# Upper parts first, pages split one by one, and one branch turned early: joined waits of an fp32 two-block transformer kernel on TensorE

## What is computed

```python
# block 1, layer i: HGRN2 + convolution mixer, then a feed-forward part
x = x + hybrid_mixer(rms_norm(x, norm_mix[i]), w_in[i], ...)
h = rms_norm(x, norm_ffn[i])
x = x + (swiglu(h, w1, w3, w2) if i == 0 else moe_swiglu(h, router_w, w1, w3, w2))  # 8 experts, 2 per token
# block 2, layer i
z = rmsnorm(x, norm_g[i]) @ w_in[i]
a = softmax(qk_0) - lam * softmax(qk_1)          # differential attention (branch A)
o_a = rmsnorm(a @ v, subln_g) * (1 - lam_init)   # needs the squares of the outcome
o_b = attention over the keys that an index picks (branch B)
o_c = gates * (compressed, selected, windowed attention) (branch C)
branches = [o_a * silu(a_g), o_b * silu(b_g), o_c * silu(c_g)]
x = x + sum(sigmoid(merge) * (branches @ w_up[i])) @ w_out[i]
x = x + (p[i] @ w_ple[i]) * sigmoid(rmsnorm(x, ple_norm_g[i]) @ w_ple_gate[i])
```

## Time and profile before

| | |
|---|---|
| median of 3 runs | 2567.53 us (2566.06 to 2570.06) |
| profiled execution | 2567.37 us, its span 2565.7 us |
| mean granted TensorE clock | 0.987 |
| TensorE busy | 2499.5 us, 17625 matmuls |
| VectorE busy | 1594.3 us |
| ScalarE busy | 1259.9 us |
| HBM read | 557.38 MB, mean 218 GB/s |

### The profile page before, as it was taken

One profiled execution on the slowest core, in us unless ns is written; L12 is line 12 of the kernel. 1 busy time (PEld: TensorE's weight loads), 2 busy tenths in 40 slices (PEclk: granted clock), 3 DMA queues, 4 the chain that ended last, 5 costly groups with the idle time before them and its releaser, 6 DMA issues.

```text
span 2565.7 us, 40739 instructions
## 1 busy us (share of the span) xinstructions
PE 2499.5 (97%) x17625; PEld 2205.2 (86%) x17625; DVE 1594.3 (62%) x1718; ACT 1259.9 (49%) x1286; POOL 5.4 (0%) x22
## 2 busy tenths in 40 slices
PE   8999999999999899999999999999999999999998
PEld 8999989989999787888887877878788898788997
DVE  5776655456766789889523334233555878557776
ACT  5555434355553576767423223233445565445555
POOL 0000000000000000000000000000000000000000
PEclk9999999999999899999999999999999999999999
DMA  7544455545442899999899789798356325555332
GB/s 240 181 164 149 141 188 182 189 165 179 160 139 91 331 391 336 350 339 363 292 335 322 262 311 342 241 334 320 132 181 193 106 89 174 181 164 172 103 119 95
DMA packets 308482, 561.07 MB, mean 219 GB/s; under 512 B 11024, under 2 KB 121040, under 8 KB 308304
## 3 DMA queue, kind: packets, MB, share of 16 engines
q1 hardware_dynamic: 307296, 556.36, 63.3%
q10 hardware_dynamic: 1008, 2.11, 0.2%
HBM read 557.38 MB, written 1.05 MB: 218 GB/s over the span
## 4 chain that ended last, share of the span: by engine, by line
PE 91%; DVE 6%; ACT 1%; issue 1%; DMA 0%; DVEq 0%; ACTq 0%
PE psG L713 61%; PE psX L713 13%; PE psG L1055 5%; PE psG L1076 2%; DVE ring_rest L2213 2%; PE psG L1378 1%; PE psG L961 1%; PE psX L1295 1%; PE psX L825 1%; PE psG L1349 1%; PE psX L702 1%; ACT tops L1509 1%; PE psX L847 0%; PE psG L1103 0%; PE psX L1246 0%
## 5 line engine op out<-in xcount | busy, mean ns | idle before, releaser
L2213 DVE TENSOR_TENSOR ring_rest<-ring,tops 128x2048 fp32r<-128x2048 f32 (+1 forms) x255 | 580.2, 2288 | 262.3 <-ACT tops L1509 260.4
L1509 ACT ACTIVATE tops<-ring 128x2048 fp32r<-128x2048 f32 (+1 forms) x255 | 483.4, 1907 | 164.5 <-PE psG L713 160.4
L713 PE MATMUL psG<-hT_rest,tops 128*128 128x256 f32 x1728 | 491.8, 285 | 0.0
L713 PE MATMUL psG<-hT_top,ring_rest 128*128 128x256 f32 x1632 | 465.2, 285 | 0.0
L713 PE MATMUL psG<-hT_top,tops 128*128 128x256 f32 x1376 | 397.9, 289 | 8.2 <-DVE hT_rest L2129 6.9
L1509 ACT ACTIVATE arena<-psG 128x512 f32<-128x512 f32 (+2 forms) x166 | 100.9, 608 | 585.7 <-PE psG L713 371.0
L713 PEld LDWEIGHTS psG<-hT_rest,tops 128*128 128x128 f32 x1728 | 334.1, 193 | 0.6
L713 PEld LDWEIGHTS psG<-hT_top,ring_rest 128*128 128x128 f32 x1632 | 315.9, 194 | 0.0
L713 PEld LDWEIGHTS psG<-hT_top,tops 128*128 128x128 f32 x1376 | 266.7, 194 | 10.9 <-DVE hT_rest L2129 7.3
L2213 DVE TENSOR_TENSOR ring_rest<-ring,tops_more 128x2048 fp32r<-128x2048 f32 x93 | 211.9, 2288 | 34.6 <-ACT tops_more L1509 34.1
L713 PE MATMUL psG<-tops,hT_top 128*128 128x512 f32 (+1 forms) x480 | 189.0, 394 | 5.4 <-issue 3.2
(11 more groups left out here) (467 smaller groups left out, 5139.7 us busy)
## 6 DMA issues: line engine op xcount, KB each, us to landing
ring<-in_expert_w_dram SPq DMA_DIRECT2D x180, 1024.0 KB, 7.3
ring<-in_w_in_dram SPq DMA_DIRECT2D x136, 1024.0 KB, 5.2
arena<-in_expert_w_dram SPq DMA_DIRECT2D x117, 1024.0 KB, 6.7
ring<-in_dense_w_dram SPq DMA_DIRECT2D x33, 1024.0 KB, 5.3
ring<-in_w_out_dram SPq DMA_DIRECT2D x16, 1024.0 KB, 5.0
ring<-in_w_up_dram SPq DMA_DIRECT2D x12, 1024.0 KB, 5.0
ring<-in_w_proj_conv_dram SPq DMA_DIRECT2D x8, 1024.0 KB, 5.1
ring<-in_w_proj_hgrn_dram SPq DMA_DIRECT2D x8, 1024.0 KB, 5.1
```

The lines of the kernel that those rows point to most:

```text
L713: mm = pe.matmul(dst, left[a], right[c], start=start and n == 0, stop=stop and n == 2)
L1509: act.activation(dst, src, func, **kw).then_inc(S[name], 1)
L2213: dve.tensor_tensor(part_of_page(rest_of(p), cols), part_of_page(raw(p), cols), part_of_page(top_of(PG.top[n]).bitcast(F32), cols), ALU.su ...
```

## The change

It has these parts:

1. The first product behind a norm goes by passes: all upper x upper products of the tile first (these wait for `hT_topped` and, for a page, `topped` alone), then the passes that need `hT_parted` or `parted` (`by_passes`, `up_first`, `tile_by_halves`).
2. In the broad jobs the three products of a page are issued page by page instead of piece by piece, with `upper_part` (waits `topped`) ahead of `both` (waits `parted`), for the g and u pages as for the down pages.
3. `top(n0)` and `rest(n0)`, the first expert page, stand between the two gathers.
4. `lead` is 2, 3, 4, 5 from tiles (1,0), (1,1), (1,2) on, instead of 2 and then 5 from (1,0).
5. `top_hT(3, ...)` and `parts(3, ...)`, the split of the activations for the 22 last steps, stand in tiles c = 3, 4 of the last broad job instead of 4, 5.
6. `mix_maps` folds one scaling into another and has no marker copy at its end (`maps_mixed` counts 2 per unit); the squares of A outcomes are read from PSUM by ScalarE (`squares_of_maps`, semaphore `o_squares`, for which `values` of the next unit waits), and the compressed keys and values are copied by ScalarE.
7. Branch A is turned, rounded and split within the last unit: TensorE ahead of the last gate tile, ScalarE ahead of `top(m+13)`, VectorE behind `rest(m+13)` and ahead of `outcome` of unit 14.

```diff
-            return 2 if n < expert_page("t", 1, 0, 0) else TOP_SLOTS - 1
+            return 2 + sum(n >= expert_page("t", j, c, 0) for j, c in ((1, 0), (1, 1), (1, 2)))
...
+            def upper_part(n, cols):
+
+                pe.wait_ge(S["topped"], PG.part[n])
+                return top_of(PG.top[n]).rearrange("p (a b) -> p a b", b=cols)
...
+            def by_passes(banks, page_n, n, norm):
+
+                for left, right in ((0, 0), (1, 0), (0, 1)):
+                    if right:
+                        pe.wait_ge(S["hT_parted"], part_of_h(norm, 2 + n))
+                    elif not left:
+                        pe.wait_ge(S["hT_topped"], part_of_h(norm, 2 + n))
+                    w = both(page_n, W)[1] if left else upper_part(page_n, W)
+                    for c in range(4):
+                        for kk in range(4):
+                            at = 4 * n + kk
+                            mm = pe.matmul(two(banks[:, c // 2, T * (c % 2):T * (c % 2) + T]), w[:, kk, P * c:P * c + P], hTp[right][:, :, at, :],
+                                           start=at == 0 and c % 2 == 0 and left == right == 0, stop=at == KD - 1 and c % 2 == 1 and right == 1)
+                return mm
...
                     if norm is not None:
-                        pe.wait_ge(S["hT_parted"], part_of_h(norm, 2 + n))
+                        mm = by_passes(psG[:, b], n0 + n, n, norm)
+                        mm.then_inc(used, 1)
+                        if mid and n == 0:
+                            mid()
+                        continue
...
+                        if j == part == 0:
+                            up_first(w)
+                            continue
...
+                def up_first(w):
+
+                    for left, right in ((0, 0), (1, 0), (0, 1)):
+                        for g in range(2):
+                            pe.wait_ge(S["hT_parted" if right else "hT_topped"], part_of_h(1, 2 + g))
+                            for c in range(2):
+                                for k in range(4 * g, 4 * g + 4):
+                                    mm = pe.matmul(two(psG[:, 0, 0, T * c:T * c + T]), w[left][:, k, P * c:P * c + P], hTp[right][:, :, k, :],
+                                                   start=left == right == k == c == 0, stop=right == c == 1 and k == KD - 1)
+                    mm.then_inc(used, 1)
...
+                            n = expert_page("t", j, c, part) + g
+                            if c == 0 and part == 0:
+                                pe.wait_ge(S["m_gath"], 2 * j + g + 1)
+                            w = upper_part(n, cols)
+                            for kk in range(per):
+                                k = per * g + kk
+                                pe.matmul(psG[:, 0, part, 0:cols], g_top[:, j % 2, k, :], w[:, kk, :], start=k == 0, stop=False)
                             if c == 0 and part == 0:
                                 pe.wait_ge(S["m_gpart"], 2 * j + g + 1)
-                            w = both(expert_page("t", j, c, part) + g, cols)
+                            for kk in range(per):
+                                pe.matmul(psG[:, 0, part, 0:cols], g_rest[:, j % 2, per * g + kk, :], w[:, kk, :], start=False, stop=False)
+                            w = both(n, cols)[1]
                             for kk in range(per):
                                 k = per * g + kk
-                                mm = three(psG[:, 0, part, 0:cols], (g_top[:, j % 2, k, :], g_rest[:, j % 2, k, :]),
-                                           [v[:, kk, :] for v in w], k == 0, k == KD - 1)
+                                mm = pe.matmul(psG[:, 0, part, 0:cols], g_top[:, j % 2, k, :], w[:, kk, :], start=False, stop=k == KD - 1)
...
+            def turn_branch(l, b):
+                pe.wait_ge(S["branch_on"], 2 * l + (2 if b == 1 else 1))
+                for c in range(4):
+                    for h in range(TH):
+                        dst = psXc[:, 4 * b + c, :] if b < 2 else psG4[:, c, :]
+                        col = (A_G, B_G, C_G)[b] + P * c
+                        mm = pe.transpose(dst[:, P * h:P * h + P], zt[:, h, col:col + P], ident)
+                mm.then_inc(S["bT_psum"], 1)
...
                     turn_exps(l, n)
+                    if n == N_UNITS - 1:
+                        turn_branch(l, 0)
                     gate_tile(l, *divmod(HALVES[n] + (n in DOUBLE), 2))
                     values(l, n)
...
                 gathered(0, 0, slim_ps)
+                top(n0)
+                state[0] += 1
                 gathered(0, 1, slim_out)
...
-                        if j == BROAD - 1 and c in (4, 5):
+                        if j == BROAD - 1 and c in (3, 4):
                             act.wait_ge(S["m_scat"], 4 * j)
-                            top_hT(3, c - 4)
+                            top_hT(3, c - 3)
...
+            def squares_of_maps(l, n):
+
+                _, qh, cs = UNITS[n]
+                act.wait_ge(S["av_read"], N_UNITS * l + n + 1)
+                for c in range(2):
+                    do(o_tmp[:, P * c:P * c + P], av_ps[:, P * c:P * c + P], ACT.Square, "o_squares",
+                       accum_out=lg[:, 9, 4 * qh + cs[c]:4 * qh + cs[c] + 1])
...
                     turned_read(l, n)
                     if n + 1 < N_UNITS:
                         softmax(l, n + 1)
+                    if n == 0:
+                        act.wait_ge(S["cmp_out"], l + 1)
+                        do(kcT[:, :, 0:NCMP], cmp_k[:, :, 0:NCMP], ACT.Copy, "cmp_sb")
+                        for c in range(4):
+                            do(vbd[32 * c:32 * c + 32, c, :], cmp_v[32 * c:32 * c + 32, c // 2, :], ACT.Copy, "cmp_sb")
                     k = PAIR_OF_STEP.get(n)
                     if n == N_UNITS - 1:
+                        branch_tops(l, 0)
                         top(m + k + 2)
                     if k:
                         gates_read(l, k)
                     if k and n < N_UNITS - 1:
                         top(m + k + 2)
+                    if UNITS[n][0] == "A":
+                        squares_of_maps(l, n)
...
                 step(dve.reciprocal(r, den[:, n % 2, 0:4]))
-                step(dve.tensor_scalar(r[:, 2:4], r[:, 2:4], nlam[:, l:l + 1], None, ALU.mult))
                 for c in range(2):
-                    go(dve.tensor_scalar(sv[:, 2 + c, :], sv[:, 2 + c, :], r[:, 2 + c:3 + c], None, ALU.mult))
+                    go(dve.tensor_scalar(sv[:, 2 + c, :], sv[:, 2 + c, :], r[:, 2 + c:3 + c], nlam[:, l:l + 1], ALU.mult, ALU.mult))
                 own()
                 for c in range(2):
                     go(dve.scalar_tensor_tensor(out=sv[:, c, :], in0=sv[:, c, :], scalar=r[:, c:c + 1], in1=sv[:, 2 + c, :],
-                                                op0=ALU.mult, op1=ALU.add))
-                own()
-                step(dve.tensor_copy(st[:, 10:11], eps), "maps_mixed")
+                                                op0=ALU.mult, op1=ALU.add), "maps_mixed")
 
             def outcome(l, n):
                 kind, qh, cs = UNITS[n]
                 k = len(cs)
                 if kind == "A":
-                    o, t = av_ps[:, 0:T].rearrange("p (c d) -> p c d", d=P), o_tmp[:, 0:T].rearrange("p (c d) -> p c d", d=P)
+                    o = av_ps[:, 0:T].rearrange("p (c d) -> p c d", d=P)
                     gated = zt[:, qh, A_G + P * cs[0]:A_G + P * cs[0] + T].rearrange("p (c d) -> p c d", d=P)
                     dve.wait_ge(S["branch_gates"], 4 * l + 4)
                     dve.wait_ge(S["av_full"], N_UNITS * l + n + 1)
-                    go(dve.tensor_copy(t, o))
-                    go(dve.tensor_tensor(gated, gated, o, ALU.mult))
-                    own()
-                    step(dve.tensor_tensor(t, t, o, ALU.mult), "av_read")
-                    step(dve.tensor_reduce(lg[:, 9, 4 * qh + cs[0]:4 * qh + cs[0] + 2], t, AX_X, ALU.add))
...
+            def branch_rests(l, i):
+                b = BRANCHES[i]
+                dve.wait_ge(S["bT_topped"], 3 * l + i + 1)
+                go(dve.tensor_tensor(b_rests[b], psXc[:, 4 * b:4 * b + 4, :] if b < 2 else psG4,
+                                     b_top[:, 4 * b:4 * b + 4, :].bitcast(F32), ALU.subtract), "bT_parted")
...
-                dve.wait_ge(S["cmp_out"], l + 1)
-                step(dve.tensor_copy(kcT[:, :, 0:NCMP], cmp_k[:, :, 0:NCMP]), "cmp_sb")
...
                     if n == N_UNITS - 1:
                         rest(m + 13)
+                        branch_rests(l, 0)
```

More of the change, by code:

```diff
@@ L78 @@
 DOUBLE = (0, 3, 6, 7, 10, 13, 14)
+BRANCHES = (0, 2, 1)
 ROUNDS = {5: (0, 1), 6: (1, 2), 7: (2, 4), 8: (4, 6), 10: (6, 8)}
@@ L2551, in experts @@
                 gathered(0, 0, slim_ps)
+                rest(n0)
+                state[0] += 1
                 gathered(0, 1, slim_out)
@@ L2570, in experts @@
                             slots(j + 1)
-                        if j == BROAD - 1 and c in (4, 5):
```

(3 more changed lines are left out.)

64 lines of the change are left out of this document (29 added, 35 removed).

## The result

The changed kernel takes 2557.68 us (median of 13 runs, 2551.04 to 2561.96), the kernel before in the same runs 2571.24 us (2565.23 to 2577.74): a ratio of 0.9947, 95% interval 0.9934 to 0.9960. It is faster by 13.6 us. The forecast was 20.3 us less, 2547, with a range up to 2557.0; it missed that range by 0.7 us. 3.8 us of the distance lie in the base, which the sum took as 2567.4 us; the other 6.7 lie in the terms.

A forecast was written before the change was run, and what follows sets the result against it. TensorE, busy 2499.5 of 2565.7 us, bounds the kernel, so only its waits and low-clock stretches can be won. Terms sum to 20.3 us: 2567.4−20.3 = 2547.1, say 2547; range 2539 to 2557.

The forecast's parts named there:

- `lead`: Expert tile (1,0): the 3.83 us wait and the low clock behind it go; 4.9 us won, bounds 2.5 to 5.5.
- rival 2: Rests put off by `lead` make VectorE late in tile (1,1) or (1,2); all 4.9 lost, 2552 us; chance 0.12.
- `parts(3)`: Layer 1's dense start: splitting one tile earlier removes a 2.44 us wait and low clock behind; 4.1 us won.
- the first tile: Layer 0: TensorE starts on upper parts 3.2 us earlier, at 11.96 instead of 15.20; 3.0 us won.
- the turned branch: Last attention unit: branch A's early turn delays the second `branch_on`, TensorE waits 2.2 us; 1.4 lost per layer, 2.8 in all.
- Rival 3: Expert tiles: every added wait costs TensorE an issue; at 0.22 us per page the time is 2576; chance 0.04.
- Rival 4: Removed waits are replaced by the next condition in line; less than 5 us stays, 2564 us; chance 0.06.
- the feed-forward start: Layer 0's FFN, `up_first`: start 1.6 us earlier, worth 0.8 to 2.5 with one low stretch less; 2.0 taken.
- maps and squares: Block 2: less VectorE work ends the `maps_mixed` wait; 4.8 us for both layers, 1.0 for the low stretch at 2361.55.
- rival 1: The clock keeps its low stretches, so only idle parts count: about 11.7 us won, 2556 us; chance 0.12.
- Experts' start: First expert tile: turn 1.2 us earlier, some 4 us of waiting spread behind pages; 0.3 won, bounds −0.5 and +1.3.
- waits inside pages: Some 190 more TensorE waits, most already fulfilled, break passes in mid-page; 1.0 us lost for all.

The follow-up runs named there:

- e3: The kernel before with only the new `lead` (3, 4, 5 over three tiles) and `parts(3)` one tile earlier: ratio 0.9962, 2559.68 against 2569.23 us.
- e4: The kernel before with only the first products behind a norm by passes: ratio 0.9979 (0.9966 to 0.9993).
- e5: The changed kernel with branch A no longer turned early, all three branches turned behind the last unit: ratio to the kernel before 0.9939, 2551.96 us.
- e6: The changed kernel with branch A still turned early by TensorE, but rounded and split late: ratio to the kernel before 0.9941.
- e10: The changed kernel with each of the eight groups of 128 products of 8 columns in two halves: ratio to the kernel before 0.9961.
- e1: The kernel before, profiled once more without an edit: span 2563.3 us.
- e9: The changed kernel with only the very first tile by pieces again, behind `hT_rest`: ratio to the kernel before 0.9956.
- e7: The changed kernel with VectorE's 1024-column product of branch A behind unit 8 instead of 4: ratio to the kernel before 0.9935.
- e8: The changed kernel with the experts as before (first page split behind both gathers, products by pieces, one wait per page): ratio to the kernel before 0.9960.
- e12: The changed kernel with VectorE's 1024-column product behind unit 8, no early turn, and narrow groups in halves: ratio to the kernel before 0.9900, 2544.53 us.
- e11: The changed kernel with VectorE's 1024-column product behind unit 8 and no early turn: ratio 0.9911, 2546.89 against 2568.13 us for the kernel before.
- e2: The changed kernel, profiled a second time without an edit: span 2557.1 us.

## Why the prediction was right or wrong

**Right, in mechanism and size** (table above, e3, e4, e5): `lead` (forecast 4.9, measured 5.6; VectorE wasn't late in tiles (1,1) and (1,2), so rival 2 falls), `parts(3)` (4.1, 4.1), block 2's first tiles (0 and 2.6; 0.0 and 2.7), layer 1's mixer (1.4, 1.7), the first tile's start (12.3 where 11.96 was forecast) and the loss by the turned branch, whose wait was forecast as 2.2 and is 2.15 us. e6 shows that its cause is the one given, the order on ScalarE and VectorE. Rival 3 falls with the constant lead from product 6970, behind the turn of tile (0,0), to the end of job 0 (0.49), and through jobs 1 to 3 (6.11 and 6.10 at products 7460 and 8800). Rival 4 holds at single places (`htok` in block 2, the experts' first turn), not for the whole.

**The step that failed: what the clock gives back.** I priced a low stretch only where a wait was removed, and took it as given back for good: part of the 3.0 for the first tile and of the 2.0 for the feed-forward start, 1.7 of the 5.5 behind `lead`, 1.0 at 2361. Behind `lead` and `parts(3)` that held in every trace. At the feed-forward start it did not: the stretch of 6.83 us stayed (323.4 in the changed kernel), and the term is 1.0 and 0.4. Behind the waits that the change makes I put the clock at nothing. The low stretches there cost 1.5 to 1.6 us each: the turned branch was forecast at −1.4 per layer and is −1.3 and −1.4 in the first execution, −2.9 and −2.9 in the second, and maps and squares are −1.0 and 0.5 in the second. In block 1's dense work I put it at nothing too. There stood a low stretch that no wait explains, right behind a long group of 128 products of 8 columns:

```profile
176.76 3.94 PE L851 MATMUL psX<-arena 128*56 128x8 f32 x128
180.63 0.58 PE L714 MATMUL psG<-hT_top,tops 128*128 128x256 f32 x1
```

TensorE's row reads busy through such a group. In the eight executions of kernels with the early start and whole groups there were 19 stretches of 3.41 us (one of 6.83 counted as two), all behind the third or fourth group of a layer, the two longest (the expectation of e10 speaks of 17 in seven; they are 16). In layer 0 there were none without the early start (before, e1, e3, e9) and at least one with it in each. This is rival 1 in part, by another way than I gave it: a start moved by 3 us changes whether a low stretch follows a narrow group of layer 0. How the start does it, no run shows. The first tile was forecast at 3.0; at 320 us it was worth 0.0 and 2.4 in the two executions of the changed kernel.

**A term that was mis-sized: maps and squares**, 5.8 forecast, 4.1 measured. The wait for `maps_mixed` went as forecast, but I didn't say what is late next: `values` of unit 5 needs maps that ScalarE reads behind the compressed unit's exponential, and that waits for VectorE, busy with the index and the 1024-column product. Before, TensorE reached this place 2 us later and at half clock, which hid it. The half clock was most of that: in e3 and e4, whose maps are those of before, the wait stands there as 1.35 us wherever this low stretch is missing (e3, first layer):

```profile
2020.90 0.85 PE L1378 MATMUL psG<-arena 128*128 128x64 f32 x6 [1.35 <-issue]
```

e7 moves that product: the wait goes, and the two parts give 8.2 us, 1.6 of them by the low stretch at 2374.78 that goes with it.

**Experts' start**, 0.3 forecast, −0.8 and −0.4 measured, of which parts 2 and 3 are +0.1 to +0.5 (e8). ScalarE began on the last page at 859.26, not 860.93 (1.05 us of that is the lead which this kernel already had), so the turn came 3.0 us earlier, 1.9 by its own part, and not 1.2. But I had the wait wrong: it doesn't spread over the pages, it stays in one piece of 4.7 us ahead of the turn, with 3.41 or 6.83 us of low clock behind. The loss by **waits inside pages** (−1.0) wasn't there.

**Open**: why a break between wide and narrow products costs 0.3 us; why a low stretch follows one wait or narrow group and not the other; what sets single runs of the kernel before anywhere from 2565 to 2577 us, of which the profiled executions only show the lower half; and e12 against e11.

## What to carry to other kernels

A wait is worth itself and at times a stretch of half clock, and the second part differs from one execution to the next: price it as a range whose lower end is the wait's own length, for the waits that a change makes as for those that it removes, and profile the same kernel twice. When TensorE is made earlier at a place, write down for the following steps which condition is fulfilled next and by how much it leads; here that would have found the 1.55 us at unit 5, and moving one VectorE operation then was worth more than the term itself missed. Before moving work of an engine ahead of a step that others wait for, as with the branch turned in the last unit, add what it puts in front of that step on each engine.

## What the runs showed of the hardware

A group of 128 products of 8 columns keeps TensorE's row busy for 3.7 us and can still be followed by 3.41 us (180.01 in the changed kernel) or 6.83 us (179.9 in e7) at the 1.2 GHz level; with the same groups in halves of 1.8 and 2.0 us none was in two executions. Two executions of one kernel with nearly the same waits differed by 6.0 us in span (2551.1 and 2557.1) by low stretches. The record of the granted clock can lack a low stretch near the program's start: in the changed kernel 16 products of 256 columns start 0.21 us apart behind 12.3 us, under a recorded 1.00. The Trainium skill ("TensorE: Matmul & The Clock Gate", "Why this matters for your kernels") asks that idle gaps between bursts of matmuls be avoided to keep the clock up. The stretches behind the waits of e2 agree with it; those behind the narrow products followed no gap.
